# Dealing modulation units out between column sums in the stretches between phases of a diffusion trunk step

## The chip, the cores and the metric

One NeuronCore of one Trainium2 chip runs the whole program. The metric is the device time of one execution in microseconds, as the median of three runs. The engines are named as in the profile: PE (TensorE matmuls), PEld (its weight loads), DVE (VectorE), ACT (ScalarE), POOL (GpSimd) and SP (the queue that issues most loads).

## The reference

Two layers of a trunk are applied to 384 tokens of width 1024 (128 context tokens and 256 latent tokens). Each layer has three parts: a SwiGLU network, a mixer of three branches, and a second SwiGLU network. Each part is wrapped in the same way:

```python
mod = silu(cond) @ ada_w[l] + ada_b[l]        # 9 vectors of 1024 for each of 2 groups of tokens
h = rmsnorm(x, g_pre) * (1 + m[3n+1]) + m[3n]
y = swiglu(h)   # or the mixer
x = x + c * m[3n+2] * rmsnorm(y, g_post)      # c is 0.5 for the SwiGLU parts, 1 for the mixer
```

Between two parts there are so two norms in a row: that of y over its 1024 columns, and, once y is added to x, that of the new x.

## The kernel before

Everything is held transposed: columns of the model on the 128 partitions (KT = 8 tiles), the 384 tokens along the free dimension. A weight unit ("w") is 128x1024 float32 numbers. SP loads it, ACT rounds it to `w_hi` (`highs`, L1070), POOL takes the rest `w_lo` (`lows`, L539), and PE makes three products of 128x384 for each pair of tiles (`product`, L599): high by high, high by low, low by high. A unit is 24 such matmuls. PE's order is that of the lists in `PHASES`: for each layer up0, down0, proj, fill, merge, out, up1, down1.

A modulation unit ("ada", `ada_unit`, L638) is 128x1024 numbers of `ada_w` for one k. It is multiplied as it was loaded by `c_col`, in four matmuls that each use a quarter of the array's columns. Eight of them make one modulation vector, summed in PSUM bank `MOD[g % 2]` (Ab or S7). When the eighth is done, DVE transposes the bank (`ada_take`, L1486), and the first unit of a group waits until the group two before it has been copied out (`ada_copied`).

In five places, called gaps here, PE passes from the last y of one part to the first h of the next: gap0, gap1 and gap2 of layer 0, gap0 and gap1 of layer 1. The first four hold `GAP` = 22 modulation units, the last holds 8. They lie in places of SBUF that are free just then (`hold_sq`, `hold`, `hold_c`, `hold_b`, `hold_a`, and four slots of the ring `raw`), and are loaded ahead. `gap(units)` on PE writes out the order: the column sums of y squared (`y_sums` into S5, 128 tokens at a time, `token_sums`, L700: three matmuls with 3 moving columns each, recorded as six); ACT takes the root, DVE the reciprocal `r_t`; `spread` (L707) lays `r_t` across the partitions in SPREAD[0]. Meanwhile four more token sums (y times x, and the gated y squared) go to X[0]. From the last one, which signals `cross_ready`, DVE works out the sum of squares of the new x without waiting for the new x itself (`grown`, L1646 to L1651), ACT and DVE make the second root, and `spread` lays it in SPREAD[1].

`joint` on DVE adds y to x tile by tile (L1638, L1639), makes the normed tile `sq` (L1661), ACT rounds it to `h_hi` (`h_highs`, L1159; it waits for the ninth modulation unit, because `hold` shares its place), and DVE takes the rest `h_lo` (`low`, L1622), which signals `h_ready`.

`by_tiles(head)` on PE takes the next part's first four weight units tile by tile as h comes: `head[0]` and `head[1]` hold k = 0 to 3 for the two column blocks that go to X[0] and X[1], `head[2]` and `head[3]` hold k = 4 to 7 for the same two. After the four, the next unit writes X[0] again and waits for `x_free[0]`, which ACT (`gate_silu`, L1166) or DVE (`proj_out`, L1756) gives when the first block has been taken out.

While y is made, ACT squares each tile of y into S5 (`squared`, L1176), scales it by the gate (`gated`, L1181) and squares that into S6 (`gated_squared`, L1192). DVE adds the squares up (`square_added`, L1718; `gated_square_added`, L1727) and makes the products with x (`with_x`, L1705, L1712). For the blocks i = 0, 1, 2 of two tiles each, ACT's `gated_squared` of both tiles comes behind the rounding of the next weight unit.

Of the kernel before, what the change touches and what calls it, by code (L numbers as in the profile page):

```python
# [12 lines left out]
KT = D // 128  # L13
# [43 lines left out]
def build(nc, io, out):  # L57
# [174 lines left out]
    with ExitStack() as ctx:  # L232
# [350 lines left out]
        def _(pe):  # L583
# [87 lines left out]
            def by_tiles(head):  # L671

                def part(u, k):
                    if k % 4 == 0:
                        pe.wait_ge(lo_ready[u.split], u.split_turn + 1)
                        if u.first:
                            pe.wait_ge(x_free[u.dest], seen.next(("xf", u.dest)))
                    for m in range(2):
                        mm = product(X[u.dest][:, m, 0:T], u, m, u.k0, k == 0, k == KT - 1, (k % 4,))
                    if k % 4 == 3:  # L680
                        mm.then_inc(unit_done[u.split], 1)

                for k in range(4):
                    pe.wait_ge(S["h_ready"], seen.next("h_ready"))
                    part(head[0], k)
                    part(head[1], k)
                for k in range(4, KT):
                    pe.wait_ge(S["h_ready"], seen.next("h_ready"))
                    part(head[2], k)
                for k in range(4, KT):  # L690
                    part(head[3], k)

            def tokens(rows):
# [13 lines left out]
                    mm = nc.tensor.transpose(dst[:, b * 128:b * 128 + 128], col[:, b:b + 1].broadcast_to([128, 128]), ident)  # L707
                mm.then_inc(S["spread_ready"], 1)

            def y_sums():  # L710

                pe.wait_ge(S["y_sq_ready"], seen.next("y_sq_ready", KT))
                pe.wait_ge(S["y_added"], seen.next("y_added", 6))
                token_sums(S5, prod[:, 0, :], True, False)
                pe.wait_ge(S["parts_ready"], seen.next("parts_ready"))
                token_sums(S5, silu[:, 0, :], False, True).then_inc(S["sum_ready"], 1)

            def gap(units):

                for u in units[:2]:  # L720
                    ada_unit(u)
                y_sums()
                pe.wait_ge(x_free[0], seen.value(("xf", 0)) + 1)
                token_sums(X[0][:, 0, 0:NB], y_sum, True, False)
                ada_unit(units[2])

                pe.wait_ge(S["r_ready"], seen.next("r_ready"))
                spread(SPREAD[0], r_t)
                token_sums(X[0][:, 1, 0:NB], silu[:, 1, :], True, False)
                pe.wait_ge(S["parts_ready"], seen.next("parts_ready"))  # L730
                token_sums(X[0][:, 0, 0:NB], part, False, True)
                pe.wait_ge(S["c_made"], seen.next("c_made", KT))
                token_sums(X[0][:, 1, 0:NB], prod[:, 1, :], False, True).then_inc(S["cross_ready"], 1)
                for u in units[3:7]:
                    ada_unit(u)

                pe.wait_ge(S["r_ready"], seen.next("r_ready"))
                spread(SPREAD[1], r_t)
                for u in units[7:]:
                    ada_unit(u)  # L740
                return by_tiles

# [316 lines left out]
        def _(act):  # L1059
# [108 lines left out]
            def y_squares(halves_done, cross):  # L1168

                def squared(u, k):  # L1170

                    if 2 <= k < 7:

                        act.wait_ge(S["y_added"], 6 * seen.value("y_phases") + k - 1)
                    dst = silu[:, 0, :] if k == 0 else prod[:, 0, :] if k == 7 else S5[:, 0:T]
                    A(dst, X[u.dest][:, k % 2, 0:T], ACT.Square).then_inc(S["y_sq_ready"], 1)  # L1176

                def gated(u, k):

                    for g, (t0, t1) in enumerate(((0, SEQ), (SEQ, T))):  # L1180
                        ins = A(y[:, k, t0:t1], X[u.dest][:, k % 2, t0:t1], ACT.Identity, scale=mG[:, k, g:g + 1])  # L1181
                    ins.then_inc(S["g_made"], 1)
                    seen.next("g_made")

                def gated_squared(k):

                    if cross:
                        act.wait_ge(S["g_made"], KT * seen.value("y_phases") + k + 1)
                        if 2 <= k < 7:
                            act.wait_ge(S["c_added"], 6 * seen.value("y_phases") + k - 1)  # L1190
                        dst = silu[:, 1, :] if k == 0 else prod[:, 1, :] if k == 7 else S6[:, 0:T]
                        A(dst, y[:, k, :], ACT.Square).then_inc(S["c_made"], 1)  # L1192

                def go(u):
                    i = u.tag[1]
                    if i < 3:
                        act.wait_ge(unit_done[u.split], u.split_turn + 1)
                        if i == 0:
                            act.wait_ge(S["mg_factor_made"], seen.next("mg_factor_made"))
                        for k in (2 * i, 2 * i + 1):  # L1200
                            squared(u, k)
                            gated(u, k)
                        return
                    act.wait_ge(S["half_done"], halves_done)
                    squared(u, 6)
                    gated(u, 6)
                    gated_squared(6)
                    act.wait_ge(unit_done[u.split], u.split_turn + 1)
                    squared(u, 7)
                    gated(u, 7)  # L1210
                    gated_squared(7)
                    act.wait_ge(S["sum_ready"], seen.next("sum_ready"))
                    root_of_sums(S5[:, 0:NB])
                    seen.next("y_phases")

                def behind(u):
                    if u.tag[1] < 3:
                        for k in (2 * u.tag[1], 2 * u.tag[1] + 1):
                            gated_squared(k)
                return go, behind  # L1220

            def head_roots():
# [243 lines left out]
        def _(dve):  # L1466
# [229 lines left out]
            def y_out(cross):  # L1696

                def with_x(u, k):

                    dve.wait_ge(S["g_made"], KT * seen.value("y_phases") + k + 1)  # L1700
                    if not cross:
                        return
                    dst = part if k else y_sum
                    for g, (t0, t1) in GROUPS:
                        ins = V.scalar_tensor_tensor(dst[:, t0:t1], X[u.dest][:, k % 2, t0:t1], mG[:, k, g:g + 1], x[:, k, t0:t1],  # L1705
                                                     MUL, MUL)
                    if k == KT - 1:
                        ins.then_inc(S["parts_ready"], 1)
                        return
                    step(ins)  # L1710
                    if k:
                        step(V.tensor_tensor(y_sum[:, :], y_sum[:, :], part[:, :], ADD))  # L1712

                def square_added(k):

                    dve.wait_ge(S["y_sq_ready"], KT * seen.value("y_phases") + k + 1)
                    if k:
                        V.tensor_tensor(silu[:, 0, :], S5[:, 0:T], silu[:, 0, :], ADD).then_inc(S["y_added"], 1)  # L1718
                        dve.wait_ge(S["y_added"], seen.next("y_added"))

                def gated_square_added(k):

                    if not cross:
                        return
                    dve.wait_ge(S["c_made"], KT * seen.value("y_phases") + k + 1)
                    if k:
                        V.tensor_tensor(silu[:, 1, :], S6[:, 0:T], silu[:, 1, :], ADD).then_inc(S["c_added"], 1)  # L1727
                        dve.wait_ge(S["c_added"], seen.next("c_added"))

                def freed(u):  # L1730

                    dve.sem_inc(x_free[u.dest], 1)
                    seen.next(("mine", u.dest))

                def go(u, i):
                    if i < 3:
                        for k in (2 * i, 2 * i + 1):
                            square_added(k)
                            with_x(u, k)
                        freed(u)  # L1740
                        for k in (2 * i, 2 * i + 1):
                            gated_square_added(k)
                        return
                    square_added(6)
                    with_x(u, 6)
                    gated_square_added(6)
                    dve.sem_inc(S["parts_ready"], 1)
                    with_x(u, 7)
                    freed(u)
                    seen.next("y_phases")  # L1750
                return go
# [446 lines left out]
```

## Time and profile before

| | us |
|---|---|
| median of three runs | 2203.36 |
| lowest and highest | 2196.66, 2206.48 |
| the profiled execution's own time | 2207.87 |
| its span | 2206.1 |
| PE busy | 2146.1 (97%) |
| PE weight loads busy | 2047.2 (93%) |
| POOL, ACT, DVE busy | 1234.2, 930.6, 893.8 |

The profile is that of one execution, and its own time is 1.8 us above its span. It is also 4.5 us above the median of the three runs, so a sum made against the profile gives a difference, and the difference is then set against the median. The mean granted TensorE clock over the span was 0.98 of full speed.

### The profile page before, as it was taken

The page shows a single profiled execution, that of the slowest core. Times are in us where ns is not written, and L with a number is a line of the kernel's source. Part 1 is how long each engine was busy: PE and PEld are TensorE (multiplying, and loading weights), DVE is VectorE, ACT ScalarE, POOL GpSimd, SP SyncE. Part 2 cuts the span into 40 slices and gives each one's busy share as a digit, 9 for nine tenths or more (in the row PEclk, how much of TensorE's full clock was granted, in tenths as well). Part 3 has the DMA queues.
Part 4 walks back from the last instruction along what each step waited for, and adds up shares of the span by engine and source line. Part 5 has one row for each costly group of instructions (what it writes and reads, how often), then busy time and mean ns, then how long its engine had stood idle before and what let it go on. Part 6 is the DMA issues. An engine that isn't in the chain of part 4 may idle for free.

```text
span 2206.1 us, 32722 instructions
## 1 busy us (share of the span) xinstructions
PE 2146.1 (97%) x13353; PEld 2047.2 (93%) x13353; DVE 893.8 (41%) x1559; ACT 930.6 (42%) x1389; POOL 1234.2 (56%) x972
## 2 busy tenths in 40 slices
PE   7999999999999999999999999999999999999998
PEld 5999998989899999999989999899898999899998
DVE  4122125446866455121351222445576564621111
ACT  3222333246776553323433233333567646422332
POOL 2666653444469464666636666453444965376663
PEclk8999999999999999999999999999999999899998
DMA  7555665423223384444554446553232245254432
GB/s 285 159 170 168 223 223 177 134 86 92 70 85 96 94 307 125 126 144 163 188 182 135 143 128 223 184 162 99 77 89 77 87 118 179 68 143 124 126 119 72
DMA packets 306925, 311.42 MB, mean 141 GB/s; under 512 B 9923, under 2 KB 285655, under 8 KB 306775
## 3 DMA queue, kind: packets, MB, share of 16 engines
q1 hardware_dynamic: 299671, 303.55, 44.1%
q10 hardware_dynamic: 7104, 5.77, 0.8%
q8 instruction: 106, 1.74, 0.3%
q14 instruction: 44, 0.36, 0.1%
HBM read 305.35 MB, written 3.93 MB: 140 GB/s over the span
## 4 chain that ended last, share of the span: by engine, by line
PE 78%; DVE 8%; ACT 7%; POOL 4%; issue 2%; DMA 1%; SPq 0%; DVEq 0%; ACTq 0%
PE X L599 55%; PE S L599 9%; PE Ab L599 5%; POOL w_lo L539 2%; PE Ab L638 1%; PE S L638 1%; PE X L700 1%; ACT w_hi L1070 1%; POOL dec L567 1%; POOL dec L566 1%; PE X L810 1%; DMA raw<-in_ada_w 1%; PE S L839 1%; ACT p L1269 1%; PE S L700 1%
## 5 line engine op out<-in xcount | busy, mean ns | idle before, releaser
L539 POOL TENSOR_TENSOR w_lo<-raw,w_hi 128x512 fp32r<-128x512 f32 (+1 forms) x872 | 1157.3, 1351 | 938.5 <-ACT w_hi L1070 929.3
L1070 ACT ACTIVATE w_hi<-raw 128x1024 fp32r<-128x1024 f32 (+1 forms) x436 | 453.5, 1041 | 663.0 <-PE X L599 629.0
L599 PE MATMUL X<-h_hi,w_hi 128*128 128x384 f32 x1600 | 538.4, 336 | 8.7 <-DVE h_lo L1622 7.9
L599 PE MATMUL X<-h_lo,w_hi 128*128 128x384 f32 x1600 | 536.3, 335 | 0.0
L599 PE MATMUL X<-h_hi,w_lo 128*128 128x384 f32 x1600 | 536.3, 335 | 0.0
L599 PEld LDWEIGHTS X<-h_hi,w_hi 128*128 128x128 f32 x1600 | 301.8, 189 | 16.2 <-DVE h_lo L1622 10.1
L599 PEld LDWEIGHTS X<-h_lo,w_hi 128*128 128x128 f32 x1600 | 301.8, 189 | 0.0
L599 PEld LDWEIGHTS X<-h_hi,w_lo 128*128 128x128 f32 x1600 | 301.7, 189 | 0.0
L1690 DVE TENSOR_TENSOR prod<-X,silu 128x768 f32<-128x768 f32 x44 | 42.1, 958 | 553.3 <-PE X L599 553.3
L599 PE MATMUL X<-act_hi,w_hi 128*128 128x384 f32 x704 | 236.3, 336 | 0.0
L599 PE MATMUL X<-act_hi,w_lo 128*128 128x384 f32 x704 | 235.9, 335 | 0.0
L599 PE MATMUL X<-act_lo,w_hi 128*128 128x384 f32 x704 | 235.8, 335 | 0.0
L599 PE MATMUL S<-h_hi,w_hi 128*128 128x384 f32 x480 | 165.5, 345 | 0.4 <-DVE proj L1523 0.4
L599 PE MATMUL S<-h_lo,w_hi 128*128 128x384 f32 x480 | 160.7, 335 | 0.0
L599 PE MATMUL S<-h_hi,w_lo 128*128 128x384 f32 x480 | 160.7, 335 | 0.0
L599 PEld LDWEIGHTS X<-act_hi,w_hi 128*128 128x128 f32 x704 | 132.7, 188 | 2.1 <-issue 2.1
L599 PEld LDWEIGHTS X<-act_hi,w_lo 128*128 128x128 f32 x704 | 132.6, 188 | 0.0
L599 PEld LDWEIGHTS X<-act_lo,w_hi 128*128 128x128 f32 x704 | 132.6, 188 | 0.0
L1718 DVE TENSOR_TENSOR silu<-S,silu 128x384 f32<-128x384 f32 x36 | 20.1, 558 | 244.8 <-ACT S L1176 244.3
L599 PE MATMUL Ab<-h_hi,w_hi 128*128 128x384 f32 x320 | 111.7, 349 | 0.7 <-DVE acc_e L1531 0.7
L599 PE MATMUL Ab<-h_hi,w_lo 128*128 128x384 f32 x320 | 107.2, 335 | 0.0
L599 PE MATMUL Ab<-h_lo,w_hi 128*128 128x384 f32 x320 | 107.2, 335 | 0.0
(398 smaller groups left out, 3133.7 us busy)
## 6 DMA issues: line engine op xcount, KB each, us to landing
raw<-in_w_in SPq DMA_DIRECT2D x124, 512.0 KB, 3.8
raw<-in_ffn_gate SPq DMA_DIRECT2D x88, 512.0 KB, 3.8
raw<-in_ffn_up SPq DMA_DIRECT2D x88, 512.0 KB, 3.8
raw<-in_ffn_down SPq DMA_DIRECT2D x80, 512.0 KB, 3.5
raw<-in_ada_w SPq DMA_DIRECT2D x48, 512.0 KB, 3.6
hold<-in_ada_w SPq DMA_DIRECT2D x29, 512.0 KB, 6.3
first_w<-in_ada_w SPq DMA_DIRECT2D x16, 512.0 KB, 10.5
hold_a<-in_ada_w SPq DMA_DIRECT2D x16, 512.0 KB, 8.0
```

The lines of the kernel that those rows point to most:

```text
L539: ins = nc.gpsimd.tensor_tensor(slot(w_lo, u)[:, part], raw_of(u)[:, part], slot(w_hi, u)[:, part], SUB)
L566: nc.gpsimd.tensor_tensor(dst[:, :, 0:b], mid, src[:, :, 0:b], SUB)
L567: nc.gpsimd.tensor_tensor(dst[:, :, b:], src[:, :, b:], mid, SUB).then_inc(S["dec_ready"], 1)
L599: mm = nc.tensor.matmul(dst, w[:, k, m * 128:m * 128 + 128], r_, start=start and k + j == 0, stop=stop and k == u.nk - 1 and j == 2)
L638: mm = nc.tensor.matmul(MOD[g % 2][32 * q:32 * q + 32, 0:256].rearrange("p (t c) -> p t c", c=32), c_col[:, u.k0, :], w[:, q, :, :], start ...
L700: mm = nc.tensor.matmul(dst[:, 0:NB], r, pick[:, NB - 1 - b:2 * NB - 1 - b], start=start and b == 0, stop=stop and b == NB - 1)
L810: mm = nc.tensor.matmul(X[n % 2][:, c, at_:at_ + k.shape[-1]], proj[64 * c:64 * c + 64, (AQ if kind == "a" else CQ) + h, b * 128:b * 128 + ...
L839: mm = nc.tensor.matmul((S5, S6)[c][:, 0:128], v, pT[:, c, j * 128:j * 128 + 128], start=j == 0, stop=j == len(kbs) - 1)
L1070: A(slot(w_hi, u), raw_of(u), ACT.Copy).then_inc(hi_ready[u.split], 1)
L1269: e = A(p[n % 2][:, c, 0:w], X[n % 2][:, c, 0:w], ACT.Exp, bias=nmax[:, n % 2, c:c + 1], accum_out=esum[:, n % 2, c:c + 1])
L1690: V.tensor_tensor(prod[:, 0:2, :], X[1][:, :, 0:T], silu[:, :, :], MUL).then_inc(x_free[1], 1)
L1718: V.tensor_tensor(silu[:, 0, :], S5[:, 0:T], silu[:, 0, :], ADD).then_inc(S["y_added"], 1)
```

## The change

In `gap`, seven modulation units are dealt out between the sums (one inside `y_sums`, one behind each of four steps), where before only one stood there after the first two; four more follow the last token sum, as before; and the rest, 11 of 22 rather than 15, follow the second spread. No unit is added or left out. In `by_tiles`, tiles 4 to 7 of h serve `head[2]` and `head[3]` in turn, as tiles 0 to 3 already served `head[0]` and `head[1]`. In ACT's and DVE's work on y, the gated square of the first tile of each block comes earlier: ahead of the rounding on ACT, and between the two tiles' other steps on DVE.

```diff
@@ by_tiles
                 for k in range(4, KT):
                     pe.wait_ge(S["h_ready"], seen.next("h_ready"))
                     part(head[2], k)
-                for k in range(4, KT):
                     part(head[3], k)
@@ y_sums, gap
-            def y_sums():
+            def y_sums(between=()):
 
                 pe.wait_ge(S["y_sq_ready"], seen.next("y_sq_ready", KT))
                 pe.wait_ge(S["y_added"], seen.next("y_added", 6))
                 token_sums(S5, prod[:, 0, :], True, False)
+                for u in between:
+                    ada_unit(u)
                 pe.wait_ge(S["parts_ready"], seen.next("parts_ready"))
                 token_sums(S5, silu[:, 0, :], False, True).then_inc(S["sum_ready"], 1)
...
                 for u in units[:2]:
                     ada_unit(u)
-                y_sums()
+                y_sums(units[2:3])
+                ada_unit(units[3])
                 pe.wait_ge(x_free[0], seen.value(("xf", 0)) + 1)
                 token_sums(X[0][:, 0, 0:NB], y_sum, True, False)
-                ada_unit(units[2])
+                ada_unit(units[4])
 
                 pe.wait_ge(S["r_ready"], seen.next("r_ready"))
                 spread(SPREAD[0], r_t)
                 token_sums(X[0][:, 1, 0:NB], silu[:, 1, :], True, False)
+                ada_unit(units[5])
                 pe.wait_ge(S["parts_ready"], seen.next("parts_ready"))
                 token_sums(X[0][:, 0, 0:NB], part, False, True)
+                ada_unit(units[6])
                 pe.wait_ge(S["c_made"], seen.next("c_made", KT))
                 token_sums(X[0][:, 1, 0:NB], prod[:, 1, :], False, True).then_inc(S["cross_ready"], 1)
-                for u in units[3:7]:
+                for u in units[7:11]:
                     ada_unit(u)
 
                 pe.wait_ge(S["r_ready"], seen.next("r_ready"))
                 spread(SPREAD[1], r_t)
-                for u in units[7:]:
+                for u in units[11:]:
                     ada_unit(u)
@@ ACT: y_squares, go and behind
                         for k in (2 * i, 2 * i + 1):
                             squared(u, k)
                             gated(u, k)
+                        gated_squared(2 * i)
                         return
...
                     if u.tag[1] < 3:
-                        for k in (2 * u.tag[1], 2 * u.tag[1] + 1):
-                            gated_squared(k)
+                        gated_squared(2 * u.tag[1] + 1)
@@ DVE: y_out, go
                     if i < 3:
-                        for k in (2 * i, 2 * i + 1):
-                            square_added(k)
-                            with_x(u, k)
+                        square_added(2 * i)
+                        with_x(u, 2 * i)
+                        square_added(2 * i + 1)
+                        gated_square_added(2 * i)
+                        with_x(u, 2 * i + 1)
                         freed(u)
-                        for k in (2 * i, 2 * i + 1):
-                            gated_square_added(k)
+                        gated_square_added(2 * i + 1)
                         return
```

## Rows read from the trace of the kernel before

**Rows 1.** The page: busy time and share of PE; the chain's shares.

```profile
PE 2146.1 (97%) x13353; PEld 2047.2 (93%) x13353; DVE 893.8 (41%) x1559; ACT 930.6 (42%) x1389; POOL 1234.2 (56%) x972
...
PE 78%; DVE 8%; ACT 7%; POOL 4%; issue 2%; DMA 1%; SPq 0%; DVEq 0%; ACTq 0%
```

**Rows 2.** Windows of first, last gap: length; PE, PEld, DVE, ACT, POOL busy; clock; DMA.

```profile
337.90:358.90 21.00, 20.04 (x220) 13.58 (x219) 14.02 (x37) 6.01 (x15) 4.25 (x4) 0.76 0.39 120
...
1893.50:1912.20 18.70, 14.02 (x107) 9.53 (x106) 12.01 (x31) 5.55 (x14) 4.47 (x4) 0.70 0.26 79
```

**Rows 3.** Timeline of PE in the first gap: start, length, work.

```profile
337.92 1.07 PE L638 MATMUL S<-hold_sq,c_col 128*32 128x256 f32 x16
...
340.77 1.08 PE L700 MATMUL S<-pick,silu 128*128 128x3 f32 x6 [0.86 <-DVEq L1747]
341.71 1.42 PE L700 MATMUL X<-pick,y_sum 128*128 128x3 f32 x6
343.06 1.08 PE L638 MATMUL S<-hold_sq,c_col 128*32 128x256 f32 x8
344.08 0.90 PE L707 MATMUL S<-con,r_t 128*128 128x128 f32 x3
344.77 1.28 PE L700 MATMUL X<-pick,silu 128*128 128x3 f32 x6
345.91 1.42 PE L700 MATMUL X<-pick,part 128*128 128x3 f32 x6
...
348.54 3.34 PE L638 MATMUL S<-hold,c_col 128*32 128x256 f32 x32
351.81 0.54 PE L707 MATMUL S<-con,r_t 128*128 128x128 f32 x3
352.28 0.64 PE L638 MATMUL S<-hold,c_col 128*32 128x256 f32 x8
...
358.90 0.44 PE L599 MATMUL X<-h_hi,w_hi 128*128 128x384 f32 x1
...
375.47 0.34 PE L599 MATMUL X<-h_hi,w_lo 128*128 128x384 f32 x1
```

**Rows 4.** Windows inside the first gap, columns as in Rows 2.

```profile
342.00:348.00 6.00, 6.00 (x33) 5.17 (x33) 1.29 (x3) 1.10 (x2) 2.49 (x2) 0.50 0.36 106
...
352.00:354.00 2.00, 2.00 (x35) 1.18 (x38) 1.63 (x5) 0.58 (x2) 0.00 (x0) 1.00 0.00 0
```

**Rows 5.** Timeline of PE near the kernel's start, units between sums.

```profile
17.63 0.64 PE L638 MATMUL Ab<-first_w,c_col 128*32 128x256 f32 x8
18.20 1.50 PE L700 MATMUL S<-pick,sq 128*128 128x3 f32 x12
19.63 0.64 PE L638 MATMUL Ab<-first_w,c_col 128*32 128x256 f32 x8
```

**Rows 6.** Window behind these, columns as in Rows 2.

```profile
21.00:27.00 6.00, 5.49 (x29) 4.57 (x29) 0.18 (x1) 0.26 (x1) 0.00 (x0) 0.50 1.04 389
```

**Rows 7.** Timeline of DVE in and behind the first gap.

```profile
350.17 0.18 DVE L1596 RECIPROCAL r_t<-r_q 128x3 f32<-128x3 f32 x1
...
354.94 0.44 DVE L1486 STREAM_TRANSPOSE ada_t<-S 128x256 f32<-128x256 f32 x1
...
355.63 0.75 DVE L1622 SCALAR_TENSOR_TENSOR h_lo<-sq,mB,h_hi 128x128 fp32r<-128x128 f32 x2
...
365.61 0.74 DVE L1622 SCALAR_TENSOR_TENSOR h_lo<-sq,mB,h_hi 128x128 fp32r<-128x128 f32 x2
...
375.58 2.06 DVE L1756 TENSOR_SCALAR proj<-X 128x768 f32<-128x768 f32 x2
```

**Rows 8.** Timeline of PE at the last gap's end.

```profile
1912.22 0.69 PE L599 MATMUL X<-h_hi,w_hi 128*128 128x384 f32 x1 [3.51 <-DVE h_lo L1622]
```

**Rows 9.** Window behind the last gap, columns as in Rows 2.

```profile
1912.30:1918.10 5.80, 5.80 (x18) 5.80 (x19) 5.63 (x14) 1.60 (x4) 0.00 (x0) 0.50 0.00 0
```

**Rows 10.** Timeline of ACT in the head behind the second gap.

```profile
853.46 0.79 ACT L1166 ACTIVATE silu<-X 128x768 f32<-128x768 f32 x1
```

## The prediction

> **What bounds the kernel now.** I read the page first: PE is busy for 97% of the span, and the chain that ended last lies on PE for 78% of it, nearly all of that in the weight products [rows 1]. So the time is PE's own work, plus what PE loses where another chain takes over. Then I read windows over the five gaps. In four of them 21 us pass, PE is busy for 20 us of it, and yet the granted clock is 0.76 on average; in the fifth, with 8 units rather than 22, it is 0.70 and PE is busy for 14.0 of 18.7 us [rows 2]. So a gap's loss is hardly idle time. It is that PE's work there runs partly at 1.2 GHz.
>
> Third, PE's timeline in the first gap beside windows inside it. Two units and six short records of the first sum come first, then a pause of 0.86 us until 340.77, when the clock is still full. Through the sums and the unit behind the pause it is at 0.50 (the window 342 to 348), and it is full again in the window 352 to 354, after three microseconds of units back to back (348.54 to 351.81) [rows 3, 4]. I read the other gaps of 22 units in the same way: their rows repeat these.
>
> Fourth, the chain that DVE sets. The second spread (351.81) waits for the cross sums, which end at 348.54, through `grown`, the second root and the reciprocal at 350.17 [rows 3, 7]. From the spread on DVE makes one tile of h after the other: the first `h_lo` ends at 356.38, the fifth at 366.35 [rows 7]. PE starts the head at 358.90 and ends it at 375.64 without a pause [rows 3]. The end of a gap is thus set by two things: PE's units, and DVE's chain behind the second spread.
>
> **The change part by part.** *Dealing out.* PE does the same 22 units and the same sums. What moves is the place of the second spread, and what the clock does meanwhile.
>
> The prices first. At full clock a unit between sums takes 18.20 − 17.63 = 0.57 us, and twelve sum records 19.63 − 18.20 = 1.43, so six take 0.71 [rows 5]. Back to back a unit takes (358.90 − 352.28)/15 = 0.44 [rows 3]. The spread takes 352.28 − 351.81 = 0.47. At half clock a unit between others takes 344.08 − 343.06 = 1.02, six sum records 345.91 − 344.77 = 1.14 to 343.06 − 341.71 = 1.35, and (348.54 − 345.91)/2 = 1.31 for the last two, the spread 0.69, and back to back a unit takes about 0.85 [rows 3]. From the end of the cross sums to the reciprocal's end it is 350.35 − 348.54 = 1.81 us at either clock, as that is ACT's and DVE's time [rows 3, 7].
>
> Unit 2 goes into the pause of 0.86 us and costs nothing (0.57). Units 3, 5 and 6 are new on the path to `cross_ready`; unit 4 takes the place that unit 2 had. Four units follow the last sum as before, so 11 stay behind the second spread rather than 15.
>
> Case A, the clock stays at 2.4 GHz through the gap. From the end of the sum at 340.77 + 0.71 = 341.48: four isolated units 2.28, four sums 2.84, one spread 0.47, together 5.59, so the cross sums end at 347.07. The reciprocal is there at 348.88, the four units behind are done at 348.8, and the second spread ends at 349.35. Before it was 352.28, so DVE's chain starts 2.9 us earlier. Then the head: unit 16, the first of its group, waits for the copy of the bank by `ada_take`, which ends 3.1 us behind the spread (354.94 + 0.44 against 352.28 [rows 7]) where PE would be there after 5 x 0.44 = 2.2 us. That new wait of 0.9 us puts the units' end 5.7 us behind the spread. It is covered: PE does tiles 0 to 3 of h until 5.7 + 8.4 = 14.1, and the fifth `h_lo` is there only at 366.35 − 352.28 = 14.07. DVE sets the end from here: 14.07 + 4 x 2.09 (twelve records of (375.64 − 358.90)/96 = 0.174 for each tile) = 22.4 us behind the spread, where it was 375.64 − 352.28 = 23.4 before. So case A gains 2.9 + 1.0 = 3.9 us per gap (for the last gap I take the same).
>
> Case B, the clock falls where it fell and comes back as before, only when units run back to back, which they do later. From 341.71: four units of 1.02, sums of 1.35, 1.14, 1.31 and 1.31, a spread of 0.69, together 9.9, so the cross sums end at 351.6, 3.1 us later than before. The four units behind take 3.4, the spread up to 0.69: it ends at about 355.6, 3.3 us late. With the 1.0 that the head gives back, case B loses 2.3 us per gap; in the last gap only one unit is left behind the sums, so the spread comes right behind the reciprocal, which stood ready 351.81 − 350.35 = 1.5 us before: 3.1 − 1.5 = 1.6, less part of what the head gives back, about 1.0 (an estimate). In the first gap DVE's small operations, not PE, set the next block (L1756 starts at 375.58 [rows 7], just behind the head), so there all 3.3 count.
>
> Case C, the clock falls, but later than before, say behind the first spread: 2.3 us at full clock, then 5.8 of sums and units, 3.4 of units and 0.5 of spread at half, which ends at 353.5, 1.2 late, less 1.0: a loss of 0.2 us.
>
> A rule of the Trainium skill speaks for case A: the page "TensorE: Matmul & The Clock Gate", in its table "Why this matters for your kernels", has PE lose its clock by idle gaps between bursts. Here the longest pause before the fall was 0.86 us, and the clock stayed at 1.2 GHz through six microseconds in which PE was busy all the time, with sums of three columns [rows 3, 4]; by that rule filling the pause would do, by the rows it may not.
>
> Another speaks against the change: "TensorEngine Tiling (Array Packing)", section "Key Properties", says that a change of tiling mode drains TensorE, and units (128x32) and sums (128x128) now alternate eight times more in a gap. Its cost is the 0.57 against 0.44 that the rows show; without it case A would be 0.5 us better per gap.
>
> *Head.* Tiles 5 to 7 of h now bring PE 2.09 us of work each rather than 1.04, so it waits for none of them. Without this edit the head would wait for each in case A; the gain is in the sums above. The other side is that `head[2]` ends 1.04 us before the head's end and not 4.2. The next unit needs X[0] free, and ACT's silu takes 0.79 [rows 10], DVE's copy 1.0 (two in 2.06 [rows 7]); with the way between engines that is from nothing to 0.3 us of wait. I take 0.2, for six heads 1.2 us.
>
> *Order of y.* ACT's and DVE's steps for the blocks 0 to 2 have 8.3 us or more per block (48 records of 0.174) and this is the same work as before in another order; the last block, whose end the gap waits for, is not touched. Nothing, at most 0.3 us for each of five phases either way, if the block before the last ends otherwise than before.
>
> **Which case.** In the first gap the fall came after a stretch with two units and a pause; the change adds one unit to it. Near the kernel's start, units between sums twice as long (0.57 in 2.0 us [rows 5]) did not keep the clock: it was at 0.50 in the window from 21 on [rows 6]. In the gap they now stand at 0.57 in 1.28 us. That lies between what lost the clock there and the units back to back that regained it. It is open per gap, and may come out otherwise in each. I take two gaps of five as case A, one as C, two as B: −7.8 + 0.2 + 4.6 = −3.0, with 1.2 for the heads −1.8 us. Against the profiled execution of 2207.87 that is 2206.1; set against the median of the runs, 2203.36 − 1.8 = 2201.6.
>
> **The rivals.** *Kept everywhere:* the clock stays full in all gaps: 5 x 3.9 − 1.2 = 18.3 us less, 2185. For it speaks that the only pause is filled; against it that six busy microseconds did not bring the clock back [rows 4]. With four of five it is 2191. In the last gap DVE's wait of 3.5 us stays [rows 8], and the 1.2 GHz behind it (5.8 us of products [rows 9]) may remain, so this case could lose 3 us of it.
>
> *Lost everywhere, the other side:* the clock falls as before in each gap and comes back one stretch of units later: 4 x 2.3 + 1.0 + 1.0 (first gap) + 1.2 = 12.4 us more, 2215.8. It decides as soon as three of five gaps go this way and none keeps its clock. The sole mechanism is that units at 1.2 GHz now stand ahead of `cross_ready`.
>
> *It changes nothing:* the fall comes a little later in most gaps (case C), or gains and losses cancel: 5 x 0.2 + 1.2 = 2.2 more, 2205.6.
>
> **How the numbers follow.** Mixed, as forecast: 0.52. Little changes: 0.20. Kept in four or five gaps: 0.14, 2185 to 2191. Lost in four or five: 0.14, 2211 to 2216. Three runs of the same kernel lie 10 us apart, so a median can tell about 0.5% (11 us) from no change. Below 2192.3 lie nearly all of "kept": 0.14. Above 2214.4 lies a third of "lost": 0.05. Within: 0.81. The range leaves out the far half of either side: 2190 to 2211.
>
> **What would show it.** A step is right if (1) windows over a gap show a granted clock of 0.9 or more in some gaps and about 0.7 in others; (2) the cross sums end 9 us behind the gap's start where the clock is full and 13 where it is not (10.6 before); (3) PE waits for `ada_t` in the middle of the units behind the second spread in gaps with full clock; (4) PE has small waits for `silu` or `proj` behind each head; (5) from the second spread's end to the head's end it is 22.4 us. The prediction is wrong if the clock behaves alike in all five gaps, if isolated units cost much more than 0.57, or if ACT's work on y becomes late in the short phase before gap1.

## The result and the profile after

| | before | after |
|---|---|---|
| median of 20 runs, us | 2201.21 | 2206.33 |
| lowest and highest | 2195.89, 2207.86 | 2200.12, 2212.19 |
| ratio, 95% interval | | 1.0027 (1.0019 to 1.0036) |
| profiled execution's span | 2206.1 | 2202.8 |
| mean granted clock of the span | 0.98 | 0.98 |

The change makes the kernel 5.1 us slower by the medians. The forecast was 1.8 us faster: the time lies in the range, the sign is wrong.

The two profiled spans stand the other way round, and that has to be understood first. Executions of one kernel lie 12 us apart, and each profile is one of them. That of the kernel before took 2207.87 us, 6.7 above its median, and that of the changed kernel 2204.61, 1.7 below its own. The profile after reached the first gap 3.7 us earlier (334.24 against 337.92). Of that, 1.7 us are there at the first product of the kernel already (38.70 against 40.41), ahead of all parts of the change. The other 2.0 arise behind it, in a stretch that holds the first head and the first block's order of y, both changed; nothing here parts their share from chance. From the first gap on, the two executions take the same time within 0.4 us (1868.6 against 1868.2), so this pair doesn't show the 5.1 us. I therefore compare from gap to gap, each counted from its own first unit. This is the page after, its busy line and the clock in 40 slices:

```profile
PE 2143.8 (97%) x13353; PEld 2038.5 (93%) x13353; DVE 882.3 (40%) x1559; ACT 930.6 (42%) x1389; POOL 1232.8 (56%) x972
...
PEclk8999999999999999999989999899999999999998
```

The windows over the five gaps after, from the first unit to the first product of the head (length; PE, PEld, DVE, ACT, POOL busy; granted clock; DMA), answer to [rows 2]:

```profile
334.30:356.40 22.10, 20.82 (x219) 12.66 (x218) 13.35 (x35) 5.27 (x13) 4.18 (x4) 0.77 0.41 132
815.00:834.40 19.40, 17.41 (x219) 10.64 (x218) 14.48 (x35) 5.54 (x13) 3.33 (x3) 0.93 0.55 175
1110.90:1134.50 23.60, 22.33 (x219) 13.60 (x218) 13.24 (x35) 5.29 (x13) 4.19 (x4) 0.71 0.41 141
1410.80:1434.10 23.30, 22.38 (x219) 13.37 (x218) 13.30 (x35) 5.28 (x13) 4.18 (x4) 0.71 0.39 135
1893.50:1909.70 16.20, 10.16 (x107) 6.54 (x106) 11.38 (x28) 4.74 (x11) 3.33 (x3) 0.80 0.31 95
```

Before, the four long gaps were alike: 21 us at 0.76. After, each is its own case. The second keeps its clock for most of the way (0.93 in 19.4 us). The third and fourth run at 0.71, which is (1 − 0.71) x 2 x 23.6 = 13.7 us at 1.2 GHz, where it was 10.1. The same list of instructions thus takes 19.4 us or 23.6 us. Nearly all of the difference is the clock; the pauses differ too, by 0.3 us ahead of the cross sums and, the other way, by 1.1 in the wait for `ada_t` behind them. PE's timeline shows how. The second gap after:

```profile
816.70 0.64 PE L638 MATMUL Ab<-hold_sq,c_col 128*32 128x256 f32 x8
817.27 0.83 PE L699 MATMUL S<-pick,silu 128*128 128x3 f32 x6
818.03 0.64 PE L638 MATMUL Ab<-hold,c_col 128*32 128x256 f32 x8
...
823.62 0.64 PE L638 MATMUL Ab<-hold,c_col 128*32 128x256 f32 x8
...
825.49 0.54 PE L706 MATMUL S<-con,r_t 128*128 128x128 f32 x3
...
830.32 1.07 PE L638 MATMUL Ab<-raw,c_col 128*32 128x256 f32 x16 [1.99 <-DVE ada_t L1490]
831.18 3.31 PE L638 MATMUL Ab<-hold_a,c_col 128*32 128x256 f32 x32
```

and the third:

```profile
1110.86 1.07 PE L638 MATMUL S<-hold_sq,c_col 128*32 128x256 f32 x16
...
1116.53 1.08 PE L638 MATMUL S<-hold,c_col 128*32 128x256 f32 x8
1117.54 0.90 PE L706 MATMUL S<-con,r_t 128*128 128x128 f32 x3
...
1124.22 1.08 PE L638 MATMUL S<-hold,c_col 128*32 128x256 f32 x8
...
1127.79 0.89 PE L706 MATMUL S<-con,r_t 128*128 128x128 f32 x3
```

The first gap lies between the two. Its clock holds up to the first spread and falls behind it:

```profile
339.76 0.65 PE L706 MATMUL S<-con,r_t 128*128 128x128 f32 x3
340.21 1.27 PE L699 MATMUL X<-pick,silu 128*128 128x3 f32 x6
341.41 1.08 PE L638 MATMUL S<-hold,c_col 128*32 128x256 f32 x8
```

A unit between sums takes 817.27 − 816.70 = 0.57 us in the one and 1117.54 − 1116.53 = 1.01 in the other (between a sum and the spread). The cross sums end 823.62 − 814.93 = 8.7 us behind the gap's start in the second gap, and 1124.22 − 1110.86 = 13.4 in the third; before it was 10.2 to 10.6 [rows 3]. All five gaps, each time counted from the gap's first unit, from the timelines of both kernels:

| gap | cross sums end | second spread ends | head starts | head ends |
|---|---|---|---|---|
| first, before / after | 10.6 / 11.9 | 14.4 / 16.2 | 21.0 / 22.2 | 37.9 / 39.1 |
| second | 10.3 / 8.7 | 14.3 / 11.0 | 20.9 / 19.5 | 37.8 / 36.7 |
| third | 10.3 / 13.4 | 14.3 / 17.8 | 21.0 / 23.7 | 37.9 / 40.6 |
| fourth | 10.2 / 13.0 | 14.3 / 17.4 | 20.9 / 23.4 | 37.9 / 40.3 |
| last | 10.3 / 8.7 | | 18.7 / 16.3 | 38.4 / 35.0 |

The ends of the five heads sum up to 191.7 us after and 189.8 before: 1.9 us more.

The new wait that the prediction named is there, and longer than it said. It is there in gaps at half clock as well (0.89, 0.88 and 0.53 us in the first, third and fourth), for which the prediction named none. These are DVE's rows in the second gap after:

```profile
825.25 0.18 DVE L1600 RECIPROCAL r_t<-r_q 128x3 f32<-128x3 f32 x1
825.47 0.56 DVE L1658 TENSOR_TENSOR x<-x,y 128x384 f32<-128x384 f32 x1
826.06 0.56 DVE L1642 TENSOR_TENSOR y<-y,S 128x384 f32<-128x384 f32 x1
826.65 0.56 DVE L1643 TENSOR_TENSOR x<-x,y 128x384 f32<-128x384 f32 x1
827.24 0.74 DVE L1665 SCALAR_TENSOR_TENSOR sq<-x,mA,S 128x128 f32<-128x128 f32 x2
...
829.73 0.44 DVE L1490 STREAM_TRANSPOSE ada_t<-Ab 128x256 f32<-128x256 f32 x1
```

The spread is done at 825.96, but DVE makes the first normed tile at 827.24 only: three steps on x and y stand in its list behind the reciprocal, 1.8 us in all. Before, the same steps were over when the spread was (it ended 1.9 us behind the reciprocal [rows 3, 7]). The copy that unit 16 waits for comes that much later as well, so PE stands for 1.99 us. Behind that pause the clock fell even in this gap (the windows are of the profile after), and the last four units took 3.2 us where they took 1.8 in the kernel before (358.90 − 357.06):

```profile
820.00:828.00 8.00, 8.00 (x112) 5.18 (x112) 5.60 (x15) 0.30 (x1) 1.92 (x2) 1.00 0.23 69
...
831.70:834.90 3.20, 3.20 (x29) 1.76 (x22) 3.10 (x8) 0.80 (x2) 0.00 (x0) 0.50 1.05 342
```

The second and the last gap, the two in which the cross sums came at 8.7 us, differ from the others in one more thing: PE has no pause before the sum of `silu`, where it has 0.3 us in the other three. They are the two gaps that the new order of y shortens (see below).

### The profile page after: what moved, and what is told of

The parts are those of the page before. It is cut to its first block, busy times and chain, and to the rows that moved or that the text cites. A ratio compares the mean times of both kernels' runs of the same rounds, so it can differ in the third digit from the quotient of the medians.

```text
span 2202.8 us, 32717 instructions
## 1 busy us (share of the span) xinstructions
PE 2143.8 (97%) x13353; PEld 2038.5 (93%) x13353; DVE 882.3 (40%) x1559; ACT 930.6 (42%) x1389; POOL 1232.8 (56%) x972
## 4 chain that ended last, share of the span: by engine, by line
PE 77%; DVE 8%; ACT 7%; POOL 4%; issue 2%; DMA 1%; SPq 1%; ACTq 0%; DVEq 0%
PE X L599 55%; PE S L599 8%; PE Ab L599 5%; POOL w_lo L539 2%; PE Ab L638 1%; ACT w_hi L1074 1%; PE S L638 1%; PE X L699 1%; POOL dec L567 1%; POOL dec L566 1%; PE X L814 1%; PE S L843 1%; DMA raw<-in_ada_w 1%; ACT p L1273 1%; SPq L516 1%
## 5 line engine op out<-in xcount | busy, mean ns | idle before, releaser
L599 PEld LDWEIGHTS X<-h_hi,w_hi 128*128 128x128 f32 x1600 | 301.7, 189 | 17.1 <-DVE h_lo L1626 9.3
```

The lines of the kernel that those rows point to most:

```text
L599: mm = nc.tensor.matmul(dst, w[:, k, m * 128:m * 128 + 128], r_, start=start and k + j == 0, stop=stop and k == u.nk - 1 and j == 2)
```

## The experiments

Each kernel was timed in five rounds beside the kernel before on the same chip; the ratio stands with its 95% interval. A difference in us is that of the medians; the ratio is close to that of the means, so the two can differ by up to 3 us. Kernels of different series are compared by their differences to the kernel before, which is looser. Gap figures are of the profiled execution of each.

**One part at a time.** Three kernels, each with one part of the change on the kernel before.

```diff
# e1: y_sums and gap as in the change; by_tiles, ACT and DVE as before
-                y_sums()
+                y_sums(units[2:3])
+                ada_unit(units[3])
...
-                for u in units[7:]:
+                for u in units[11:]:
```

> The kernel before with the dealing out of units alone. Theory 1 (one unit between sums lengthens the way to the cross sums and doesn't keep the clock: in most gaps it falls where it fell, and comes back one stretch later): 5 to 9 us slower than before, all of the change's loss; the cross sums end 12 to 13.4 us behind the gap's start in gaps where the clock fell (10.25 before), 8.7 where it didn't, and the time at 1.2 GHz in such a gap is 13.7 us rather than 10.2. Theory 2 (the loss is in the head or the order of y: waits for X[0], later rounding on ACT): within 2 us of before.

2211.74 against 2204.28: ratio 1.0047 (1.0029 to 1.0065), 7.5 us slower (10 by the ratio). No gap of the profiled execution kept its clock, and that execution was itself slow for its kernel (2219.26 us); the windows over its first, third and fourth gap read

```profile
337.80:361.40 23.60, 22.33 (x219) 13.44 (x218) 13.23 (x35) 5.28 (x13) 4.18 (x4) 0.71 0.37 128
...
1119.60:1143.20 23.60, 22.33 (x218) 13.38 (x218) 13.25 (x35) 5.23 (x13) 4.12 (x4) 0.71 0.41 146
1419.60:1443.30 23.70, 22.42 (x219) 13.61 (x218) 13.34 (x35) 5.31 (x14) 4.20 (x4) 0.71 0.42 147
```

that is 2.6 us longer each than before [rows 2], with the cross sums' end at 12.3 to 13.7 us. The dealing out alone loses at least what the whole change loses, and theory 2 falls.

```diff
# e2: by_tiles alone
                     part(head[2], k)
-                for k in range(4, KT):
                     part(head[3], k)
```

> The kernel before with tiles 4 to 7 of h serving two units alone. Theory 1: 0 to 1 us faster, since before PE is not kept waiting by DVE in the four long gaps; only the last gap, where it is, gains some. Theory 2 (the block behind the head waits for X[0], which is given 3 us later): 3 to 5 us slower, with waits of PE for silu or proj behind each of six heads.

2203.86 against 2204.28: 1.0001 (0.9988 to 1.0013). In the four long gaps it takes 20.8 to 21.0 us to the head, and the heads end at 37.9, as before. The last head ends at 36.6 rather than 38.4, but 1.5 us of that are there at its start (17.2 against 18.7), ahead of what this part changes. The wait for X[0] that I had charged with 1.2 us can't be told from nothing, and neither can a gain (−2.6 to +2.9 us).

```diff
# e5: ACT and DVE alone
+                        gated_squared(2 * i)
                         return
...
-                        for k in (2 * u.tag[1], 2 * u.tag[1] + 1):
-                            gated_squared(k)
+                        gated_squared(2 * u.tag[1] + 1)
# and on DVE gated_square_added(2 * i) between the two tiles' steps, as in the change
```

> The kernel before with the new order of the gated squares on ACT and DVE alone. Theory 1 (the blocks before the last have slack, and the last is untouched): within 1.5 us of before, the starts of the gaps' sums unchanged. Rival (the rounding on ACT comes 0.5 us later in each block and PE meets it in the short phase): 2 us slower or more, with new waits of PE for w_lo.

2200.71 against 2202.68: 0.9986 (0.9976 to 0.9996), 2.0 us faster (3.1 by the ratio), a little more than theory 1 allowed. The rival's sign is wrong; so was my "nothing". In the short phase before the second gap ACT was late in the kernel before, which ACT's timeline there shows:

```profile
816.48 0.50 ACT L1192 ACTIVATE S<-y 128x384 f32<-128x384 f32 x1 [2.20 <-DVE silu L1727]
816.91 1.04 ACT L1070 ACTIVATE w_hi<-raw 128x1024 fp32r<-128x1024 f32 x1
817.86 0.48 ACT L1176 ACTIVATE S<-X 128x384 f32<-128x384 f32 x1
```

and with the new order:

```profile
813.80 0.50 ACT L1192 ACTIVATE S<-y 128x384 f32<-128x384 f32 x1 [0.16 <-DVE silu L1727]
814.23 1.05 ACT L1070 ACTIVATE w_hi<-raw 128x1024 fp32r<-128x1024 f32 x1
816.21 0.47 ACT L1176 ACTIVATE S<-X 128x384 f32<-128x384 f32 x1 [0.93 <-PE X L599]
```

ACT's second gated square waited 2.20 us for DVE's sum of the first, with a rounding and the next block's first square queued behind it. That square starts 1.0 us before the gap in the kernel before (817.86, gap at 818.85) and 2.0 us before it here (816.21, gap at 818.18), and PE's pause in the sums shrinks from 0.88 to 0.18 us in the second and last gap. Two gaps of 0.7 us are 1.4 of the 2.0. In the profiled execution the gain there was larger, as the clock fell later too: in the second gap it was 0.82 over 18.5 us, and the head ended at 35.5 us rather than 37.8, in the last gap at 35.4 rather than 38.4. So the pause that this part takes away may bear on the clock as well; one profile can't show it.

**What one unit in the pause is worth.**

```diff
# e3: gap of the kernel before, and
-                y_sums()
+                y_sums(units[2:3])
...
-                ada_unit(units[2])
+                ada_unit(units[3])
...
-                for u in units[3:7]:
+                for u in units[4:8]:
...
-                for u in units[7:]:
+                for u in units[8:]:
```

> The kernel before with one unit in the pause of y_sums, the next units moved up by one each, and 14 rather than 15 behind the second spread; nothing stands newly before the cross sums but in the pause. Theory 1: the unit is free there and the second spread comes where it came, so 0.4 us per gap less behind it, and in some executions the clock falls later: 2 to 4 us faster. Rival (more units early only move work, the gap ends with DVE's chain): within 1 us of before.

2200.26 against 2204.28: 0.9987 (0.9976 to 0.9998), 3 to 4 us faster, as theory 1 said. In the profiled execution two of the five gaps ended at 36.1 rather than 37.9; in those the granted clock was 0.82 over 19.0 us, which is 6.8 us at 1.2 GHz rather than 10.1. So the unit in the pause is the good part of the dealing out; the three that follow on the way to the cross sums turn 3 to 4 us of gain into a loss of 7.5 or more.

**Enough units to keep the clock.** The change deals out five units; the seven that its description counts include the two that stand ahead of the sums, as before. Here the changed kernel has nine dealt out rather than five:

```diff
-                y_sums(units[2:3])
-                ada_unit(units[3])
+                y_sums(units[2:5])
+                some(units[5:7])          # ada_unit for each
                 token_sums(X[0][:, 0, 0:NB], y_sum, True, False)
-                ada_unit(units[4])
+                some(units[7:8])
                 spread(SPREAD[0], r_t)
                 token_sums(X[0][:, 1, 0:NB], silu[:, 1, :], True, False)
-                ada_unit(units[5])
+                some(units[8:10])
                 token_sums(X[0][:, 0, 0:NB], part, False, True)
-                ada_unit(units[6])
+                some(units[10:11])
...
                 add_to_x(0)
+                ada_take(units[7])        # DVE; no longer behind tile 1 of h
```

> The changed kernel with 3, 2, 1, 2, 1 units in the slots (9 rather than 5 dealt out), four behind the cross sums as before, 7 behind the second spread, and the first group's copy by ada_take moved ahead of the cross sums. Theory 1 (what keeps the clock is how much of the time the units fill, not that the sums follow one another without a pause): the clock stays at 2.4 GHz through the gap in all five gaps, the cross sums end about 10.5 us behind the gap's start, no wait for ada_t, 1.5 us per gap less than before: 6 to 9 us faster than before, 11 to 14 faster than the change. Rival (units ahead of the cross sums cost their length whatever the clock): 2 us per gap slower than the change, about 15 us slower than before.

2197.12 against 2204.28: 0.9966 (0.9953 to 0.9979), 7.2 us faster than before and about 12 faster than the change. The windows over the four long gaps, the first two shown:

```profile
339.20:356.60 17.40, 16.02 (x219) 9.91 (x218) 11.54 (x31) 5.13 (x13) 4.20 (x4) 1.00 0.52 170
817.00:834.20 17.20, 15.92 (x219) 9.88 (x218) 10.92 (x28) 4.57 (x11) 3.33 (x3) 1.00 0.49 161
```

The clock is full from end to end in all four; in the last gap, with its wait for `h_lo`, it is 0.85. With four more units ahead of them the cross sums end at 10.4 to 10.6 us, 2.4 to 3 us sooner than in the change's third and fourth gap. This tells the two theories apart: more work on the same way made it shorter, which only the clock can do. (The copy of the first group, moved here too, is tried alone in e6.) What is left is DVE's chain: PE waits 14.1 us for `h_lo` in all.

**The copy that unit 16 waits for.**

```diff
# e6: the changed kernel, and on DVE
+                ada_take(units[7])
                 add_to_x(2)
                 dve.wait_ge(S["spread_ready"], ...)
...
-                    if k == 1:
-                        ada_take(units[7])
```

> The changed kernel with DVE's copy of the first modulation group moved from behind the second tile of h to ahead of the second spread. The change's profile shows 4.3 us of PE's waits for that copy in the middle of the units, and behind the longest one (2.0 us) the clock fell once. Theory 1: those waits go, 1 to 4 us faster than the change, so 1 to 4 us slower than before; the way to the cross sums (12 to 13.4 us in gaps where the clock fell) stays. Rival (the wait for the copy is the main part of the loss): level with before or faster.

2206.88 against 2202.68: 1.0016 (1.0007 to 1.0025). The change had 1.0027 (1.0019 to 1.0036) beside another series of runs, so the copy is worth about 1 to 2 us of the 5; the intervals overlap, and a gain isn't shown. The waits for `ada_t` are gone from the list. In the profiled execution the clock fell in all four long gaps (0.70 to 0.76) and the cross sums ended at 11.0 to 13.1 us. The rival falls.

**Units where they cost least.**

```diff
# e7: as e4, with other numbers of units per slot
+                y_sums(units[2:5])
                 token_sums(X[0][:, 0, 0:NB], y_sum, True, False)
+                some(units[5:7])
                 spread(SPREAD[0], r_t)
+                some(units[7:8])
                 # the three token sums, nothing between them
+                some(units[8:11])
                 spread(SPREAD[1], r_t)
+                some(units[11:])
```

> The kernel with two per slot, but with its units where they cost least: 3 in the pause, none behind the next sum, 2 and 1 around the first spread, none between the three later sums, 3 behind the cross sums, 10 behind the second spread. The same early copy. Theory 1 (each unit ahead of the cross sums costs its 0.43 us once the clock is kept, and the eight that are left ahead are enough to keep it): cross sums end 9.0 us behind the gap's start rather than 10.5, clock full in most gaps, 1.0 to 1.5 us per gap less than with two per slot: 12 to 15 us faster than before. Rival (three sums in a row, at most a spread between, let the clock fall as before): about 10 us at 1.2 GHz in most gaps and within 3 us of before.

2186.81 against 2202.68: 0.9930 (0.9918 to 0.9943), 15.9 us faster than before and about 21 faster than the change. Its windows, the first two gaps and the last:

```profile
337.50:353.60 16.10, 15.63 (x219) 9.87 (x219) 12.29 (x31) 5.25 (x13) 4.15 (x4) 1.00 0.48 160
814.50:830.40 15.90, 15.51 (x219) 9.90 (x218) 11.89 (x28) 4.75 (x11) 3.35 (x3) 1.00 0.42 135
...
1879.40:1895.00 15.60, 9.30 (x106) 6.43 (x106) 11.59 (x28) 4.61 (x11) 3.31 (x3) 0.88 0.30 95
```

The cross sums end at 8.8 to 8.9 us and the heads at 34.3 to 34.4, 3.5 us less per gap than before (4.1 in the last, where the clock is 0.88). Three sums in a row didn't cost the clock in this execution. This kernel has the lowest median of the study, though e8 and e10 can't be told from it. They try what is left of it, and e9 takes back the head.

```diff
# e8: e7, and DVE adds y to x two tiles ahead, not three
-                add_to_x(2)
...
-                    if k + 3 < KT:
-                        add_to_x(k + 3)
+                    if k + 2 < KT:
+                        add_to_x(k + 2)
```

> The front-loaded kernel, and DVE adds y to x only two tiles ahead of the norm rather than three (the addition of tile 2 no longer stands before the first normed tile). Theory (with the clock kept, DVE's chain behind the reciprocal sets the gap's end, and the fifth h_lo counts): another 0.8 to 1.1 us per gap, 3 to 5 us faster than the front-loaded kernel. Rival (the products or the units set the end): within 1 us of it.

2188.26 against 2202.68: 0.9933 (0.9920 to 0.9947), no gain over e7. In the fourth gap, where the clock held, the head ended at 33.7 rather than 34.4, so the chain did get shorter. In the first three the clock fell for a while; PE's timeline in the first gap:

```profile
348.33 1.89 PE L638 MATMUL Ab<-hold_c,c_col 128*32 128x256 f32 x16
350.15 0.90 PE L706 MATMUL S<-con,r_t 128*128 128x128 f32 x3
```

and the window over the same stretch, with the clock at 0.50:

```profile
348.50:351.70 3.20, 3.20 (x29) 1.32 (x23) 2.20 (x8) 0.30 (x1) 0.00 (x0) 0.50 0.36 137
```

I took that for the effect of PE's short pause before the second spread, and gave it a fourth unit there. The rows above don't bear this out: the two units from 348.33 on already run at half clock (1.89 us, where the same two take 1.05 in e7), so the fall comes ahead of the spread and of any pause there, right behind the three sums in a row. And e7 has that pause, 0.38 us, in each long gap of its profile and kept its clock.

```diff
# e10: e8, with four units behind the cross sums
-                some(units[8:11])
+                some(units[8:12])
-                some(units[11:])
+                some(units[12:])
```

> The front-loaded kernel with the additions two tiles ahead, as in the lagging kernel, and four units rather than three behind the cross sums, to fill the pause of up to 1.8 us before the second spread, behind which the clock fell in three gaps for 3.4 us. Theory: the clock stays full in the four long gaps, 1 to 4 us faster than the front-loaded kernel, 17 to 20 us faster than before. Rival (the gap's end is set elsewhere): within 1 us of the front-loaded kernel.

2189.33 against 2201.50: 0.9940 (0.9925 to 0.9954). The clock held in three of four long gaps, and their heads end at 33.7; in the second it fell and the head ended at 35.4. PE's timeline there has no pause, and the clock falls with the first unit behind the sums:

```profile
822.26 0.81 PE L699 MATMUL X<-pick,prod 128*128 128x3 f32 x6
823.00 1.08 PE L638 MATMUL S<-hold,c_col 128*32 128x256 f32 x8
823.85 1.93 PE L638 MATMUL S<-hold_c,c_col 128*32 128x256 f32 x16
```

The median doesn't show a gain. The theory's part on the chain holds per gap (0.7 us), its part on the time doesn't.

```diff
# e9: e7 with by_tiles as before
                     part(head[2], k)
+                for k in range(4, KT):
                     part(head[3], k)
```

> The front-loaded kernel with the head as before (tiles 4 to 7 serve one unit, then the other unit has all four). Theory (where DVE's chain sets the gap's end, serving two units per tile gives PE work while it waits): 0.5 to 1.5 us per gap lost, 2 to 6 us slower than the front-loaded kernel, so 10 to 14 us faster than before. Rival (the head's order is worth nothing here either, as it was alone): within 1 us of the front-loaded kernel.

2192.56 against 2201.50: 0.9953 (0.9939 to 0.9968), 9 us faster than before and so 5 to 7 us slower than e7. Per gap the head ends 0.5 to 0.6 us later (34.8 to 35.0), since PE now waits for each late tile, as the weight loads' timeline in the second gap shows:

```profile
843.94 0.19 PEld L599 LDWEIGHTS X<-h_hi,w_hi 128*128 128x128 f32 x1 [0.43 <-DVE h_lo L1626]
845.25 0.19 PEld L599 LDWEIGHTS X<-h_hi,w_hi 128*128 128x128 f32 x1 [0.31 <-DVE h_lo L1626]
846.56 0.19 PEld L599 LDWEIGHTS X<-h_hi,w_hi 128*128 128x128 f32 x1 [0.31 <-DVE h_lo L1626]
```

That is 2.8 us of the 5 to 7 over five gaps. In three of its gaps the clock also fell for a while (0.90 on average over the gap), which e7's profile doesn't have. As in e8 and e10 it fell between the last of the three sums and the second spread. Up to there e7 to e10 have the same list of instructions, and in their profiles they lost the clock in none, three, three and one of four long gaps. What decides between them isn't shown; that three sums in a row can cost the clock, the rival put up for e7, is likely.

## Why the prediction was wrong

- **The step that failed** is the price of case A, "gains 2.9 + 1.0 = 3.9 us per gap", and in it the wait for the copy, "It is covered". In the profile after, the second gap gained 1.1 us (37.8 to 36.7), though its cross sums ended even sooner (8.7 us) than forecast (9.1). The wait was 2.0 us rather than 0.9, since 1.8 us of DVE's own steps stand behind the reciprocal (first normed tile 12.3 us behind the gap's start rather than 11.5), and the clock fell behind it, which cost 1.4 more. So the head started at 19.5 us, not at the forecast's 17.1, and the fifth `h_lo` (26.2, its row ends at 841.12) was there before PE wanted it (19.5 + 8.4 = 27.9): PE's units set the end, not DVE's chain. The forecast of that chain itself was nearly right. From the second spread's end to the head's end it is 23.1 us in e4 and e7, where the clock is full and the wait is gone; forecast 22.4; in this gap 25.7.
- **The step "Which case"** reads "I take two gaps of five as case A, one as C, two as B". The one execution profiled has this very mix: the second and last gap are A, the first is C (cross sums at 11.9 us, where the prediction's case C has 353.5 − 0.5 − 3.4 − 337.92 = 11.7), the third and fourth are B. With the measured prices the same mix comes out at −1.1 − 3.4 + 1.2 + 2.8 + 2.4 = +1.9 us rather than −3.0, so the prices alone turn the sign. Of the difference of 4.9 us, 3.3 are case A's and 1.0 is case C's (1.2 rather than 0.2).
- **What stays open.** The median lies 5.1 us above that of before, and this execution doesn't show that much. That in most executions more gaps go the way of B is likely: e1 kept the clock in no gap of its profile, e6 in none of the four long ones, and both medians are slower. How many gaps fall in each of the twenty executions, no trace shows.
- **Case B's price was right, but for one gap.** Forecast 2.3 us per gap and the cross sums 13.7 us behind the gap's start; measured 2.8 and 2.4, and 13.4 and 13.0. The isolated unit at 0.57 and 1.02 was right too (0.57, 1.01). In the first gap "all 3.3 count" was wrong: PE's wait for `proj` behind that head shrank from 0.88 to 0.32 us and took up part of the delay.
- **The rival "it may not"** of the rows against the page's rule was the right one. The Trainium skill, page "TensorE: Matmul & The Clock Gate", table "Why this matters for your kernels", ties the fall to idle gaps between bursts. In the change the clock fell in the third gap although its longest pause ahead of the fall was 0.29 us; here the trace doesn't agree with idle time as the only cause.
- **The order of y** was put at nothing because the last block was untouched. It was late all the same, behind a wait of ACT in the block before: −2 us.
- **The head** was charged with 1.2 us and shows 0 (−2.6 to +2.9 us by the interval). Its gain appears only where the clock is kept (e9).
- The three parts alone sum to 1.0047, 1.0001 and 0.9986, together 1.0034, and the change measured 1.0027: they add up within their intervals.

That the time lies in the range says little for the mechanism: the range was 21 us wide, and it would have held nearly every mix but the two ends.

## What to carry to other kernels

If units of work are to be put among sums of a few moving columns, first find out from the granted clock whether the mixture keeps it. Where it doesn't, each inserted unit costs nearly double (1.01 against 0.57 us) and delays whatever waits for the sums; where it does, the same stretch gets shorter although it holds more (e4). Put filler where the engine would pause, around the first result's round trip, rather than between the last sums before a signal to another engine: that was worth some 8 us from e4 to e7, though the clock was then lost in some gaps of e8 to e10. Look at several executions before a verdict, as one profile had the wrong sign here. And when a signal comes earlier, hang the next engine's chain on all that it waits for, its own list of steps included.

## What the runs showed of the hardware that was not expected

- PE busy without a pause doesn't keep its clock: with one unit after each sum of three columns it fell in the first, third and fourth gap after, with no pause over 0.3 us ahead of the fall, and the units then took 1.01 us, and with nine units dealt out rather than five it was 1.00 in all four long gaps.
- Where the units do keep the clock, a pause can lose it: behind a wait of 1.99 us at 830.32, with units before it, the granted clock was 0.50 from 831.7 to 834.9. Pauses of 0.38 us among units cost e7 nothing.
- With the same list of instructions up to the cross sums, the five gaps of one execution differ by up to 4.7 us (8.7 to 13.4 us), all but 0.3 us of it by the clock. In e7, whose profile keeps the clock, five runs lie within 3.5 us (2186.43 to 2189.89), where twenty of the changed kernel lie 12 us apart.
- Behind three sums in a row, with the clock full up to their end (8.8 to 8.9 us), it fell before the second spread in seven of the twelve long gaps of e8, e9 and e10 and in none of e7's four; in e10's second gap (823.00) PE had no pause in the gap at all.
